# Expert weights in 2 MB chunks of 16 KB per partition, with the contraction renumbered by four rows

## What is computed

```python
def ec_moe(h, w_r, w1, w3, w2):
    B, n, D = h.shape
    cap = max(1, EC_CAPACITY * n // N_EXPERTS)
    aff = jax.nn.softmax((h @ w_r).astype(jnp.float32), axis=-1)
    gate, idx = lax.top_k(jnp.swapaxes(aff, 1, 2), cap)
    xin = jax.vmap(lambda hb, ib: hb[ib])(h, idx)
    hid = jax.nn.silu(jnp.einsum('becd,edf->becf', xin, w1)) * jnp.einsum('becd,edf->becf', xin, w3)
    ye = jnp.einsum('becf,efd->becd', hid, w2) * gate[..., None].astype(h.dtype)
    return jax.vmap(lambda yb, ib: jnp.zeros((n, D), h.dtype).at[ib.reshape(-1)].add(yb.reshape(-1, D)))(ye, idx)
```

## Time and profile before

| | us |
|---|---|
| median of 3 runs | 2952.15 |
| profiled execution, own time | 2956.25 |
| its span, first to last instruction | 2953.6 |
| TensorE busy in the span | 2644.9 (90%) |
| VectorE busy | 793.2 (27%) |
| ScalarE busy | 498.5 (17%) |
| DMA, 663.81 MB, mean | 225 GB/s |

### The profile page before, as it was taken

One profiled execution on the slowest core, in us unless ns is written; L12 is line 12 of the kernel. 1 busy time (PEld: TensorE's weight loads), 2 busy tenths in 40 slices (PEclk: granted clock), 3 DMA queues, 4 the chain that ended last, 5 costly groups with the idle time before them and its releaser, 6 DMA issues.

```text
span 2953.6 us, 30831 instructions
## 1 busy us (share of the span) xinstructions
PE 2644.9 (90%) x13301; PEld 1556.7 (53%) x13301; DVE 793.2 (27%) x1661; ACT 498.5 (17%) x1042; POOL 55.6 (2%) x85
## 2 busy tenths in 40 slices
PE   8999999999999999999989898888999997666665
PEld 5678878578864444444443243334457873232322
DVE  2625411435412453341130011012343311000001
ACT  1620010230021031221031111113021221000001
POOL 1000000000002000000000000001100000000000
PEclk9999999999999999999989999999999998777877
DMA  8645444554455211212139999999422348999995
GB/s 281 205 159 164 162 143 143 199 171 161 162 188 138 77 37 57 72 57 71 61 141 415 421 421 421 421 422 354 125 77 100 128 143 340 421 421 421 421 421 246
DMA packets 201019, 663.81 MB, mean 225 GB/s; under 512 B 13426, under 2 KB 58784, under 8 KB 151732
## 3 DMA queue, kind: packets, MB, share of 16 engines
q1 hardware_dynamic: 192912, 641.97, 56.5%
q0 software_dynamic: 7776, 19.81, 2.8%
q10 hardware_dynamic: 196, 0.06, 0.0%
HBM read 660.67 MB, written 9.57 MB: 227 GB/s over the span
## 4 chain that ended last, share of the span: by engine, by line
PE 68%; DMA 25%; ACT 3%; DVE 3%; issue 0%; ACTq 0%; DVEq 0%
PE ps L474 40%; DMA ring<-in_w_e 24%; PE ps L495 7%; PE ps L1052 5%; PE ps L655 5%; PE ps L1007 1%; PE ps L1033 1%; PE ps L901 1%; PE ps L590 1%; PE ps L856 1%; PE ps L923 1%; PE ps L869 1%; PE ps L844 1%; ACT normed L1873 1%; DMA ring<-in_w_ada 1%; PE ps L521 1%
## 5 line engine op out<-in xcount | busy, mean ns | idle before, releaser
L474 PE MATMUL ps<-normed,ring 128*128 128x256 f32 (+1 forms) x3456 | 948.5, 435 | 13.9 <-ACT normed L1873 10.1
L1052 PE MATMUL ps<-ring,arena 128*32 128x256 f32 (+1 forms) x4608 | 632.3, 531 | 216.4 <-DMA ring<-in_w_e 210.4
L474 PEld LDWEIGHTS ps<-normed,ring 128*128 128x128 f32 x3456 | 659.3, 192 | 281.8 <-issue 208.1
L1052 PEld LDWEIGHTS ps<-ring,arena 128*32 128x32 f32 (+1 forms) x4608 | 203.9, 134 | 625.7 <-DMA ring<-in_w_e 324.3
L474 PE MATMUL ps<-arena,ring 128*128 128x256 f32 (+1 forms) x832 | 253.3, 462 | 1.4 <-DVE small L1169 1.4
L495 PE MATMUL ps<-ring,normed 128*128 128x512 f32 x512 | 222.1, 592 | 0.0
L474 PEld LDWEIGHTS ps<-arena,ring 128*128 128x128 f32 x832 | 156.3, 190 | 89.4 <-issue 73.8
L1250 DVE COPY arena<-ps 128x256 f32<-128x256 f32 (+1 forms) x102 | 56.0, 554 | 418.7 <-PE ps L474 174.7
L495 PEld LDWEIGHTS ps<-ring,normed 128*128 128x128 f32 x512 | 96.4, 190 | 117.2 <-issue 117.2
L655 PE MATMUL ps<-arena,ring 128*128 128x256 f32 x704 | 152.3, 379 | 0.0
L655 PEld LDWEIGHTS ps<-arena,ring 128*128 128x128 f32 x704 | 133.8, 190 | 18.2
(11 more groups left out here) (236 smaller groups left out, 1802.0 us busy)
## 6 DMA issues: line engine op xcount, KB each, us to landing
ring<-in_w_e SPq DMA_DIRECT2D x384, 1024.0 KB, 17.9
ring<-in_w_in SPq DMA_DIRECT2D x56, 1024.0 KB, 7.3
ring<-in_w_ada SPq DMA_DIRECT2D x48, 1024.0 KB, 6.8
ring<-in_ffn_w_up SPq DMA_DIRECT2D x88, 512.0 KB, 5.4
ring<-in_ffn_w_down SPq DMA_DIRECT2D x22, 1024.0 KB, 5.0
ring<-in_dil_w_qkv SPq DMA_DIRECT2D x18, 1024.0 KB, 4.9
ring<-in_sb_w_qkv SPq DMA_DIRECT2D x12, 1024.0 KB, 13.4
ring<-in_w_branch SPq DMA_DIRECT2D x12, 1024.0 KB, 5.0
```

Source lines behind the costliest of these rows:

```text
L474: ins = mm(o[:, 0:n], slots[k // 4][:, k % 4, f * P:(f + 1) * P], src[:, k, 0:n], start=k == 0, stop=k == kts - 1)
L1052: ins = mm(o[w * g:w * g + w, 0:cols], lhs(2 * c + j), slot[:, j, g * cols:(g + 1) * cols], start=c == 0 and j == 0, stop=c == KT // 2 - 1 ...
```

## The change

Each expert matrix is cut by `rows(w, j)` into pieces of j rows per partition. With j = 4 a chunk has 512 rows of the matrix, 16 KB in one piece per partition, 2 MB in all, and it takes two neighbouring slots of the ring: the list has an empty entry behind it, and SyncE skips that. SyncE waits until both old slots are read, and issues one DMA. TensorE waits once for a chunk of 2 MB, and frees its two slots together. `w1` and `w3` have j = 4 in both layers; `w2` has 4 in the first layer and stays at 2 in the second (`DOWN_RUN`), where a piece of the turned hidden values has only 256 columns. The contraction is renumbered: step 4c+j has row 512c+4p+j, so `gather` and, in the first layer, `expert_turn` read their operand with a step of four elements instead of two. The number of matmuls and transposes, their shapes and the bytes moved stay as they are.

```diff
+DOWN_RUN = (4, 2)
...
-    def rows(w):
-        for r0 in range(0, D, 2 * P):
-            out.append([(w[r0:r0 + 2 * P, :].rearrange("(p j) n -> p (j n)", j=2), 0, 1, SLOT, 1)])
+    def rows(w, j):
+
+        for r0 in range(0, D, j * P):
+            out.append([(w[r0:r0 + j * P, :].rearrange("(p j) n -> p (j n)", j=j), 0, 1, j // 2 * SLOT, 1)])
+            out.extend([[]] * (j // 2 - 1))
...
-            for w, of in (("w_e1_2", e), ("w_e3_2", e), ("w_e2_2", e - 1)):
+            for w, of, j in (("w_e1_2", e, 4), ("w_e3_2", e, 4), ("w_e2_2", e - 1, DOWN_RUN[i])):
                 if 0 <= of < N_EXPERTS:
-                    rows(a[w][i][of])
+                    rows(a[w][i][of], j)
...
-        HTP = HT.rearrange("p t (c m j) -> p t c j m", m=P, j=2)
+        HTP = HT.rearrange("p t (c m j) -> p t c j m", m=P, j=4)
...
-                                    ins = mm(o[:, n * P:(n + 1) * P], HTP[:, ST * q + j, k // 2, k % 2, :],
+                                    ins = mm(o[:, n * P:(n + 1) * P], HTP[:, ST * q + j, k // 4, k % 4, :],
...
-                def expert_rows(o, lhs):
-
-                    for c in range(KT // 2):
-                        (slot, loaded, count), = next_chunks(1)
+                def expert_rows(o, lhs, run):
+
+                    for c in range(KT // run):
+                        n = state["chunk"]
+                        (_, loaded, count), *_ = next_chunks(run // 2)
                         pe.wait_ge(loaded, count)
-                        slot = slot.rearrange("p (j n) -> p j n", j=2)
-                        for j in range(2):
+                        slot = ring[:, (n % NSLOT) * SLOT:(n % NSLOT + run // 2) * SLOT].rearrange("p (j n) -> p j n", j=run)
+                        for j in range(run):
                             for g in range(groups):
...
-                        if c < KT // 2 - 1:
+                        if c < KT // run - 1:
                             ins.then_inc(chunk_used, 1)
                             used[0] += 1
-                            freed_at.append(-used[0])
+                            freed_at.extend([-used[0]] * (run // 2))
                     ins.then_inc(banks.filled, 1)
-                    chunks_done(1)
+                    chunks_done(run // 2)
...
-                    halves = HN[:, 0:cols].rearrange("p (c m j) -> p c j m", m=P, j=2)
+                    run = DOWN_RUN[i]
+                    parts = HN[:, 0:cols].rearrange("p (c m j) -> p c j m", m=P, j=run)
                     for n in range(cols // P):
-                        ins = nc.tensor.transpose(o[:, n * P:(n + 1) * P], halves[:, n // 2, n % 2, :], ident)
+                        ins = nc.tensor.transpose(o[:, n * P:(n + 1) * P], parts[:, n // run, n % run, :], ident)
...
             for n, pieces in enumerate(chunks):
+                if not pieces:
+                    continue
+                units = max(1, pieces[0][3] // SLOT) if pieces[0][2] == 1 else 1
                 if n >= NSLOT:
 
-                    at = freed_at[n - NSLOT]
+                    at = freed_at[n + units - 1 - NSLOT]
...
-                slot = ring[:, (n % NSLOT) * SLOT:(n % NSLOT + 1) * SLOT]
+                slot = ring[:, (n % NSLOT) * SLOT:(n % NSLOT + units) * SLOT]
```

More of the change, by code:

```diff
@@ L1042, in _ @@
                 cols = D // groups
-                def expert_rows(o, lhs):
-                    for c in range(KT // 2):
-                        (slot, loaded, count), = next_chunks(1)
+                def expert_rows(o, lhs, run):
+                    for c in range(KT // run):
+                        n = state["chunk"]
+                        (_, loaded, count), *_ = next_chunks(run // 2)
                         pe.wait_ge(loaded, count)
-                        slot = slot.rearrange("p (j n) -> p j n", j=2)
-                        for j in range(2):
+                        slot = ring[:, (n % NSLOT) * SLOT:(n % NSLOT + run // 2) * SLOT].rearrange("p (j n) -> p j n", j=run)
+                        for j in range(run):
                             for g in range(groups):
-                                ins = mm(o[w * g:w * g + w, 0:cols], lhs(2 * c + j), slot[:, j, g * cols:(g + 1) * cols],
-                                         start=c == 0 and j == 0, stop=c == KT // 2 - 1 and j == 1)
-                        if c < KT // 2 - 1:
+                                ins = mm(o[w * g:w * g + w, 0:cols], lhs(run * c + j), slot[:, j, g * cols:(g + 1) * cols],
+                                         start=c == 0 and j == 0, stop=c == KT // run - 1 and j == run - 1)
+                        if c < KT // run - 1:
                             ins.then_inc(chunk_used, 1)
                             used[0] += 1
-                            freed_at.append(-used[0])
+                            freed_at.extend([-used[0]] * (run // 2))
                     ins.then_inc(banks.filled, 1)
-                    chunks_done(1)
+                    chunks_done(run // 2)
                 def expert_up(e):
@@ L1065, in expert_up @@
                         pe.wait_ge(*banks.due)
-                        expert_rows(o, lambda k: XIN[:, k, e, 0:w])
+                        expert_rows(o, lambda k: XIN[:, k, e, 0:w], 4)
                     hidden_read[e] = read_by("v")
@@ L1087, in turned @@
                         return HE[e % 2][:, n, g * w:(g + 1) * w]
-                    expert_rows(o, turned)
+                    expert_rows(o, turned, DOWN_RUN[i])
                     expert_out[e] = read_by("a")
@@ L1142, in _ @@
                         sp.wait_ge(chunk_used, -at)
-                slot = ring[:, (n % NSLOT) * SLOT:(n % NSLOT + 1) * SLOT]
+                assert n % NSLOT % units == 0
+                slot = ring[:, (n % NSLOT) * SLOT:(n % NSLOT + units) * SLOT]
                 for src, c0, k, w, _ in pieces:
```

## The result

The changed kernel takes 2968.95 us (median of 4 runs, 2968.33 to 2969.51) against 2953.23 us for the kernel before beside it: a ratio of 1.0054, 95% interval 1.0036 to 1.0071. It is slower by 15.7 us where 9.3 us less were forecast. The time fell outside the stated range (2939 to 2965), above the 2963.4 us of rival A. The profiled execution has a span of 2967.4 us against 2953.6.

The account below looks back on a forecast made before the run. The expert loops were taken as bound by the weight stream, at 420 GB/s. Longer packets -11.9, later restart +2.6, end waits 0, step of four 0: -9.3 us, giving 2942.9 us from 2952.15; range of 8 in 10, 2939 to 2965.

Parts of the forecast that it names:

- rival A: In gather, the step of four halves the weight-load rate, 0.24 us a pair: +11.3 us, 2963.4 us; chance 22%.
- What bounds the kernel: Both expert loops end when the weight bytes have come, at 420 GB/s; TensorE does not set the time there.
- part 1: Expert loops: fewer, longer packets save 78 ns in each of 152 chunks of 2 MB, 11.9 us (11.1 to 12.5).
- The line through two rates: Weight stream: 421 GB/s with 8 KB packets and 387 with 2 KB ones give 9.1 ns a packet.
- Part 2: Start of each loop: two slots freed together delay the stream 1.74 and 0.89 us, 2.6 us lost, at least 0.9.
- Part 3: Ends of both expert loops: TensorE's waits for 2 MB chunks cost zero.
- Part 4: gather and expert_turn: a step of four costs 0; at the high end a gather's pair goes from 0.12 to 0.24 us.
- B: Expert weights: 16 KB pieces don't travel as one packet each; +1.2 to +2.6, some 2954 us; chance 15%.
- C: Expert weights: 16 KB packets are slow, 4.3 us more for each of 152 chunks, +650 us; chance 3%.
- D: Expert loops: longer idle pieces lower TensorE's clock and a few us are lost, 2946 to 2955; chance 8%.
- the recurrence: Around a gather: queue empty at 19.6 us after a landing, new bytes at 16.6; with slow gathers 24.3, 4.7 us lost.

Follow-up runs that it names:

- experiment 3: Kernel before with 2 MB chunks in two slots, one DMA and wait each, but 8 KB packets, old numbering and step of two: 2953.80 us, ratio 1.0001.
- experiment 1: Changed kernel with only gather's weight operand back at a step of two: 2945.37 us, ratio 0.9973 against the kernel before.
- big_8k: The kernel of experiment 3: 2 MB chunks with packets of 8 KB, old numbering and step of two; 2953.80 us, ratio 1.0001 against the kernel before.
- experiments 3 and 9: Experiment 3, and the changed kernel with each later gather of the first layer cut in two: 2954.70 us, ratio 1.0006 against the kernel before.
- after_step2: The kernel of experiment 1: changed kernel with the step of two in gather; 2945.37 us, ratio 0.9973 against the kernel before.

## Why the prediction was wrong

**What bounds the kernel, and part 1: right.** The packets became 16 KB; their rate went to 426 or 427 GB/s where nothing disturbed it (428 forecast). The line through two rates, 9.1 ns a packet, held for a length that the trace had not shown: 9.4 ns were measured (experiment 3). The two loops of experiment 1 are 6.4 and 4.8 us shorter than those of big_8k, 11.2 in all where part 1 gave 11.9. By the 3 cycles a packet of the Trainium skill ("DMA: Bandwidth & Descriptors", Why small descriptors are slow) it would have been an estimated 5 us; the measured loops decide for the rows.

**Part 2: right in place, small in size.** big_8k has the loops 1.6 and 1.3 us longer, 2.9 in all, where 2.6 less up to 1.4 for signals were forecast. Its time can't be told from no change. The least of 0.9 us, by which larger issues would fill the slow start, is not borne out.

**Part 3: right.** Behind the first loop TensorE still waits for `w_ada`: before, it was idle for 1.59 and 3.50 us ahead of the first two groups at L590; now it is not idle ahead of the first, and 3.23 us ahead of the second. So the 1.74 us of later work are hidden, as the sum had it. The second loop is 3.5 us shorter in experiment 1, near the 3.8 of the sum, which leaves little room for a loss at its end.

**Part 4: the step that failed.** It took 0 for the step of four in `gather`, between the ends 0 and a doubling, "as the nearest row (`gather` itself) shows only 4 ns for the first step". The other end was true: 330 ns a load and 0.235 us a pair. The row chosen was near in its place, but not in its mechanism. A cost that comes in with a threshold (how many wanted elements share a piece) can't be read off one point on the near side. Nor was the other evidence good: the 68 ns in the transposes, given in favour of A, hardly grew (209 to 213 ns). What that load waits for, and which of the two operands of a transpose it is, no row told and no run has settled.

**Rivals B, C and D: out.** The packets carry 16 KB (against B) and move at 426 GB/s (against C), and the granted clock over the first loop, 1557 to 2020 us, is 1.00 (against D). Single falls of it do cost a us or two where they meet other work, as experiments 3 and 9 show.

**Rival A: right in mechanism, too small in its holes.** It gave +5.1 and +1.4 for the two first gathers; +5.0 and +1.4 were measured. It gave 4.7 us for each hole. The first loop of after against after_step2 is 19.5 us longer, 6.5 for each of three. The landings say the same: the chunks behind the three holes land 11.2, 12.8 and 11.8 us after the ones before them, where 4.9 is the pace. The mis-sized term is the restart: the recurrence put 1.2 us from a freed slot to the first bytes, and counted the queue's end from a landing. But a landing is itself late by the way back. The changed kernel's DMA view of 1630 to 1650 us, in slices of 0.5 us, and the time from issue to landing of the chunk issued at 1641.1:

```profile
GB/s 328 426 459 492 492 262 426 492 426 524 164 66 66 66 0 0 33 0 0 0 0 0 0 0 459 0 360 295 328 524 459 360 492 426 360 492 492 360 459 328
...
DMA to landing us min/median/max: 7.9/7.9/7.9
```

The bytes thin out from 1635 on, though the last queued chunk lands only at 1637.8 (issued at 1621.9, 15.9 us to landing), and they come back at 1642, a microsecond behind the issue. Of the 7.9 us the bytes take 4.9 at the usual pace, and the way out and back 3.0. With that, TensorE is through the next chunk 22.7 us after the landing (it starts on the landed one at 1618.21, and is through the next at 1637.39 + 3.5 = 1640.9), the chunk issued then lands at 30.6, and was due at 5 x 4.9 = 24.5: 6.1 us, near the 6.3 of this hole and the 6.5 on average. In the other two holes the chunk needs 9.4 and 8.9 us to land; what makes these longer is open. The term would also have left 1.2 us of slack in part 2 instead of 3.0: still no loss, but near to one.

The chances were fair in kind: A had 22%, and the forecast 52%. The range ended at 2965 because A was priced at 2963.4; with holes of 6.5 us A would have come out at 2969.

## What to carry to other kernels

When a layout change is made for one engine's sake, look at every reader and writer whose step it changes, and count how many wanted elements each 16-byte piece of SBUF still holds. For the 32-bit floats of these kernels two were enough (a pair of load and matmul 0.120 us, a copy 0.62 us), and one took nearly twice as long (0.236 and 1.10 us), for TensorE's weight loads as for ScalarE's writes. Put the step on the PSUM side if there is a copy on the way (0.59 us with it). And in a stage bound by its DMA queue, other work costs nothing as long as each uninterrupted stretch is shorter than what the queue still holds, less the round trip, 3 us for these chunks: 7.7 us cost nothing here, 15.1 us cost 6.5. That each microsecond beyond the limit counts in full is worked out, not swept. So cut the stretch before you cut the work, and leave TensorE time to catch up between the pieces.

## What the runs showed that was not expected

- A step of four or eight elements costs a weight load of 128 x 128 floats 330 and 336 ns against 196 with a step of two and 192 with none. In the second layer's `gather(0)` part of this hides behind the low clock: its 32 pairs took 7.73 us (granted clock 0.78) against 6.33 before (0.59), while a later gather of 32 at the full clock took 7.62 against 3.93.
- A transpose of data read with a step of four is no slower than with a step of two (0.75 against 0.74 us for four).
- ScalarE's copy of 128 x 512 floats takes 1.10 us when it writes single floats 512 bytes apart, 0.62 when it writes pairs, and 0.59 when it writes side by side but reads PSUM with a step of four.
- Chunks of 2 MB with 8 KB packets bring nothing (420 GB/s); with 16 KB packets it is 426 to 427.
- A DMA queue that ran empty comes back slowly: with 1 MB chunks the first lands 5.0 to 5.4 us after its issue and the second 3.6 to 3.9 us behind it, where 2.5 is the pace.
